# Interleaving the 128-column slices of the stationary operands of a two-layer decoder trunk

## The chip, the cores and the metric

The kernel runs on one core of a Trainium2 chip. The metric is the device time of one execution in microseconds (us); lower is better. The time before the change is 1608.19 us, the median of three runs that lie between 1607.14 and 1608.36 us.

## The reference

A causal decoder trunk of two layers works on x of shape 256 x 2048 in float32. Layer 0 is retention with 8 heads, layer 1 a causal pooling mixer with 4 groups; each ends with an embedding gated by a sigmoid.

```python
def retention_branch(xn, w_in, w_out):
    q, k, v, g = split(xn @ w_in)            # 2048 -> 8 heads x (256 + 256 + 512 + 512)
    ...                                      # rotary q, k; decayed scores; y = scores @ v; group norm
    return (silu(g) * y) @ w_out             # 4096 -> 2048

def pool_branch(xn, w_in, w_group, scale, w_out):
    u, g = split(xn @ w_in)                  # 2048 -> 4096 + 4096
    ...                                      # window means of u minus u -> d
    mixed = einsum('bsgc,gce->bsge', d, w_group) * scale      # 4 groups of 1024 x 1024
    return (mixed * silu(g)) @ w_out         # 4096 -> 2048

def reference(...):
    for i in range(2):
        h = h + branch_i(rms_norm(h, norm_i))
        gate = sigmoid(rms_norm(h, ple_norm[i]) @ ple_w_gate[i])
        h = h + gate * (p[i] @ ple_w_proj[i])
    return rms_norm(h, final_norm)
```

## The kernel before, in words

Every large product has 256 rows (two token tiles t of 128) and streams its weights once from memory. A float32 value is split in two float32r parts, hi and lo, and a product is three matmuls: x_hi by w_hi (L304), x_hi by w_lo (L305) and x_lo by w_hi (L306). The x part is the stationary operand: a slice of 128 columns (the tokens of one tile) by 128 partitions (channels), loaded anew before each matmul. The weight part is the moving operand of 512 columns.

The work is cut in 552 units. A unit holds two channel blocks of 128 by 512 output columns of weights. For each unit ScalarE writes w_hi (L567, a cast of 128x1024), VectorE writes w_lo (L800, a subtraction of 128x1024) and TensorE runs 12 matmuls: two tiles t, two channel blocks b, three products. Four units of w_hi and w_lo are held in a ring (RING = 4). TensorE waits for a unit on `lo_ready`, ScalarE waits before it overwrites a slot on `unit_used`. The unit order is written out by hand in the loops of each engine.

The stationary operands before the change lie in buffers `[P, blocks, SEQ]`, so the 128 columns of a slice are neighbours in the partition's memory:

- `xa_hi`, `xa_lo` (16 blocks x 256): the input of all projections. It is read by 3 passes per head and 4 per group, each of 8 units.
- `oT_hi`, `oT_lo` (8 blocks x 256): the gated branch output, transposed, read by the output projections (8 units per head, 16 per group).
- `xb_hi`, `xb_lo` (16 blocks x 256): the input of the two gate products (32 units each).
- `dT_hi`, `dT_lo`: the window means (8 units per group). `pT_hi`, `pT_lo`: the embedding inputs (4 units per layer).

Who fills them: `h_transposes` transposes a chunk of four blocks of h into two PSUM banks (L327, 8 transposes), `stream_hi` on ScalarE writes the hi part block by block (L587, 4 x 128x256), and `stream_lo` on VectorE writes the lo part, reading PSUM and the hi part (L839, 4 x 128x256). `xT_ready` tells TensorE that a chunk is whole; TensorE waits for it before it reads the chunk, and before the next chunk's transposes. `y_hi_part` and `y_lo_part` (L615, L914, 128x512) fill `oT` for a head, `m_hi_part` and `m_lo_part` (L656, L967, 128x256) for a pooling group.

At the start the order on TensorE is: transposes of chunks 0 and 1, unit 0, transposes of chunk 2, unit 1, transposes of chunk 3, units 2, 3 and on.

Of the kernel before, what the change touches and what calls it, by code (L numbers as in the profile page):

```python
# [92 lines left out]
def trunk(nc, stream, x, pT, gains, pool_scale, final_gain, rope, decay, band, counts, ident, out):  # L93
    with ExitStack() as ctx:
# [22 lines left out]
        w_raw = sb("w_raw", [P, RAW, PIECE * COL], F32)  # L117
        w_hi = sb("w_hi", [P, RING, UNIT * COL], F32R)
        w_lo = sb("w_lo", [P, RING, UNIT * COL], F32R)
        xa_hi = sb("xa_hi", [P, KD, SEQ], F32R)  # L120
        xa_lo = sb("xa_lo", [P, KD, SEQ], F32R)
        oT_hi = sb("oT_hi", [P, KG, SEQ], F32R)
        oT_lo = sb("oT_lo", [P, KG, SEQ], F32R)
        h = sb("h", [P, TT, D], F32)
        emb = sb("emb", [P, TT, D], F32)
        pT_hi = sb("pT_hi", [P, 2, KP, SEQ], F32R)
        pT_lo = sb("pT_lo", [P, 2, KP, SEQ], F32R)
# [30 lines left out]
        dT_hi = at("dT_hi", 8, [P, KG, SEQ], F32R)  # L158
        dT_lo = at("dT_lo", 16, [P, KG, SEQ], F32R)
# [136 lines left out]
        def _(pe):  # L296
            def products(t, s, pair, hi, lo, k0, first, last):

                for b in range(UNIT):
                    xh = hi[:, k0 + b, t * P:(t + 1) * P]  # L300
                    xl = lo[:, k0 + b, t * P:(t + 1) * P]
                    wh = w_hi[:, s, b * COL:(b + 1) * COL]
                    wl = w_lo[:, s, b * COL:(b + 1) * COL]
                    pe.matmul(acc[pair][t][:], xh, wh, start=first and b == 0, stop=False)  # L304
                    pe.matmul(acc[pair][t][:], xh, wl, start=False, stop=False)  # L305
                    mm = pe.matmul(acc[pair][t][:], xl, wh, start=False, stop=last and b == UNIT - 1)  # L306
                return mm
# [179 lines left out]
            def close(layer, base, seg, ou):  # L487

                for c in range(EMB_U):
                    if c >= 2:  # L490
                        pe.wait_ge(e_read, layer * NC + c - 1)
                    if c == 1 and layer == 0:
                        pe.wait_ge(v_ready, HEADS)
                    if c == 0 and layer == 0:
                        pe.wait_ge(p_split, 1)
                    unit(c, base, "AC"[c % 2], pT_hi[:, layer], pT_lo[:, layer], 0, True, True, seg)
# [12 lines left out]
                z0 = layer * NC  # L509
                last = EMB_U + NC * ou + GATE_U  # L510
                if layer == 1:
                    last -= RING
                for u in range(EMB_U, last):
                    c, k = divmod(u - EMB_U, ou)
                    z, kz = divmod(u - EMB_U - NC * ou, KD_U)
                    if c < NC:
                        if k == 0 and c in (1, 2):
                            pe.wait_ge(e_read, z0 + c + 2)
                        if k == 0 and c == 3:
                            pe.wait_ge(h_ready, h0 + 1)  # L520
                        unit(u, base, "BACB"[c], oT_hi, oT_lo, k * UNIT, k == 0, k == ou - 1, seg)
                    else:
                        if kz == 0 and z < 3:
                            pe.wait_ge(h_ready, h0 + z + 2)
                        if kz == 0 and z == 3:
                            pe.wait_ge(z_read, z0 + 2)
                        if z == 0 and kz % 2 == 0:
                            pe.wait_ge(xT_ready, NC * (2 * layer + 1) + kz // 2 + 1)
                        unit(u, base, "ACBC"[z], xb_hi, xb_lo, kz * UNIT, kz == 0, kz == KD_U - 1, seg)
                    for cc in range(NC):  # L530
                        if u == EMB_U + ou * (cc + 1):
                            h_transposes(2 * layer + 1, cc)
                        if cc < NC - 1 and layer == 0 and u == EMB_U + NC * ou + KD_U * (cc + 1) + 1:
                            h_transposes(2, cc)
# [22 lines left out]
        def _(act):  # L557
# [54 lines left out]
            def y_hi_part(hd):  # L612
                act.wait_ge(yT_done, hd + 1)
                for b in range(2):
                    act.copy(oT_hi[:, 2 * b:2 * b + 2, :], side[b][:].rearrange("p (k n) -> p k n", n=SEQ)  # L615
                             ).then_inc(yT_hi, 1)

            def emb_out(layer, c, base):
# [22 lines left out]
            def d_hi_part(n, c):  # L641
                for b in range(2):
                    act.wait_ge(d_scaled, n * 2 + (b + 1))
                    act.copy(dT_hi[:, 4 * c + 2 * b:4 * c + 2 * b + 2, :], d_tmp[:, 2 * b:2 * b + 2, :]).then_inc(d_hi_ready, 1)

            def pg_sigmoid(n, pair, done, first):
                act.wait_ge(unit_used, done)
# [5 lines left out]
            def m_hi_part(n, k0, c):  # L653
                act.wait_ge(mT_done, n + 1)
                for j in range(4):
                    cp = act.activation(oT_hi[:, 4 * c + j, :], side[j // 2][:, (j % 2) * SEQ:(j % 2 + 1) * SEQ], ACT.Copy,  # L656
                                        scale=pscale[:, bass.ds(k0 + j, 1)])
                    if j % 2:
                        cp.then_inc(mT_hi, 1)

            def head(hd, base, first, landings):
                o = 0 if first else NC * RO_U
                for u in range(3 * KD_U + o):
# [129 lines left out]
        def _(dve):  # L793
# [169 lines left out]
            def m_lo_part(n, k0, c):  # L963
                for j in range(4):
                    if j % 2 == 0:
                        dve.wait_ge(mT_hi, n * 2 + (j // 2 + 1))
                    ins = dve.scalar_tensor_tensor(  # L967
                        out=oT_lo[:, 4 * c + j, :], in0=side[j // 2][:, (j % 2) * SEQ:(j % 2 + 1) * SEQ],
                        scalar=pscale[:, bass.ds(k0 + j, 1)], in1=oT_hi[:, 4 * c + j, :].bitcast(F32),
                        op0=ALU.mult, op1=ALU.subtract)  # L970
                ins.then_inc(mT_ready, 1)

            def head(hd, base, first):
                o = 0 if first else NC * RO_U
                for u in range(3 * KD_U + o):
# [279 lines left out]
```

## Time and profile before

| | |
|---|---|
| Median of three runs | 1608.19 us |
| The profiled execution's own time | 1607.45 us |
| Its span, first to last instruction | 1605.6 us |
| TensorE matmul busy | 1584.2 us, 7240 instructions |
| TensorE weight load busy | 1317.9 us, 7240 instructions |
| VectorE busy | 988.2 us |
| ScalarE busy | 727.0 us |
| Mean granted TensorE clock | 0.998 |

Matmul and weight load overlap: they are two rows for one engine. A record's duration includes the time in which an operand travels, and neighbouring records overlap, so the distance between two starts tells more than a duration. The span is 1.9 us shorter than the execution's own time.

### The profile page before, as it was taken

To read this page: it belongs to the slowest core of one execution; us is meant where nothing else is said; L and a number is where in the kernel's file an instruction comes from. 1 tells how busy PE (TensorE), PEld (TensorE's weight loads), DVE (VectorE), ACT (ScalarE), POOL (GpSimd) and SP (SyncE) were. 2 spreads that over 40 slices of the span, in tenths; PEclk is the share of its full clock that TensorE was granted. 3 is DMA by queue.
4 is the path that set the end of the run, shared out by engine and by line. 5 is a ranking of instruction groups with operands and counts; after the bars stand their busy time and mean duration, and the time that the engine had idled before them with its cause. 6 is when DMAs were issued, how large, how long until landed. Compare 5 with 4: busy or idle time off the path is not lost.

```text
span 1605.6 us, 19583 instructions
## 1 busy us (share of the span) xinstructions
PE 1584.2 (99%) x7240; PEld 1317.9 (82%) x7240; DVE 988.2 (62%) x1218; ACT 727.0 (45%) x888; POOL 5.1 (0%) x13
## 2 busy tenths in 40 slices
PE   7999999999999999999999999999999999999997
PEld 6888888888888888888888888888888888888885
DVE  5676666657566666757756555645565555556565
ACT  6444444444443444445655444334434443445553
POOL 0000000000000000000000000000000000000000
PEclk9999999999999999999999999999999999999999
DMA  9444554545455554555455554555555555455551
GB/s 356 172 171 182 184 187 176 187 180 183 183 183 183 183 183 159 207 183 195 166 197 197 186 186 174 198 187 184 183 184 182 200 188 182 179 217 183 184 185 77
DMA packets 42806, 299.24 MB, mean 186 GB/s; under 512 B 4848, under 2 KB 4864, under 8 KB 7312
## 3 DMA queue, kind: packets, MB, share of 16 engines
q1 hardware_dynamic: 41408, 292.60, 50.5%
q0 software_dynamic: 1072, 5.06, 0.8%
q10 hardware_dynamic: 288, 1.05, 0.2%
q8 instruction: 26, 0.43, 0.1%
q14 instruction: 12, 0.10, 0.0%
HBM read 296.60 MB, written 2.10 MB: 186 GB/s over the span
## 4 chain that ended last, share of the span: by engine, by line
PE 98%; DVE 1%; DMA 0%; ACT 0%; issue 0%; SPq 0%; ACTq 0%
PE accB L304 11%; PE accB L305 11%; PE accB L306 11%; PE accA L304 10%; PE accC L304 10%; PE accA L306 10%; PE accA L305 10%; PE accC L305 10%; PE accC L306 10%; PE side L327 2%; DMA h<-in_x_dram 0%; PE side L369 0%; PE side L367 0%; PE side L368 0%; PE side L416 0%; PE side L417 0%
## 5 line engine op out<-in xcount | busy, mean ns | idle before, releaser
L800 DVE TENSOR_TENSOR w_lo<-w_raw,w_hi 128x1024 fp32r<-128x1024 f32 x552 | 669.4, 1222 | 418.7 <-ACT w_hi L567 413.6
L567 ACT CAST w_hi<-w_raw 128x1024 fp32r<-128x1024 f32 x552 | 579.6, 1055 | 620.4 <-PE accB L306 263.7
L304 PE MATMUL accA<-w_hi,xa_hi 128*128 128x512 f32 x512 | 201.4, 393 | 0.9 <-DVE w_lo L800 0.9
L306 PE MATMUL accA<-w_hi,xa_lo 128*128 128x512 f32 x512 | 199.8, 390 | 0.0
L305 PE MATMUL accA<-w_lo,xa_hi 128*128 128x512 f32 x512 | 199.8, 390 | 0.0
L304 PE MATMUL accC<-w_hi,xa_hi 128*128 128x512 f32 x384 | 150.7, 392 | 0.0
L305 PE MATMUL accC<-w_lo,xa_hi 128*128 128x512 f32 x384 | 149.5, 389 | 0.0
L306 PE MATMUL accC<-w_hi,xa_lo 128*128 128x512 f32 x384 | 149.4, 389 | 0.0
L304 PE MATMUL accB<-w_hi,xa_hi 128*128 128x512 f32 x384 | 149.4, 389 | 0.0
L305 PE MATMUL accB<-w_lo,xa_hi 128*128 128x512 f32 x384 | 149.4, 389 | 0.0
L306 PE MATMUL accB<-w_hi,xa_lo 128*128 128x512 f32 x384 | 149.4, 389 | 0.0
L304 PEld LDWEIGHTS accA<-w_hi,xa_hi 128*128 128x128 f32 x512 | 96.6, 189 | 20.9 <-DVE w_lo L800 1.1
L306 PEld LDWEIGHTS accA<-w_hi,xa_lo 128*128 128x128 f32 x512 | 96.4, 188 | 20.2
L305 PEld LDWEIGHTS accA<-w_lo,xa_hi 128*128 128x128 f32 x512 | 96.5, 188 | 19.5
L304 PE MATMUL accB<-w_hi,oT_hi 128*128 128x512 f32 x256 | 99.8, 390 | 0.0
L305 PE MATMUL accB<-w_lo,oT_hi 128*128 128x512 f32 x256 | 99.6, 389 | 0.0
L306 PE MATMUL accB<-w_hi,oT_lo 128*128 128x512 f32 x256 | 99.6, 389 | 0.0
L306 PEld LDWEIGHTS accC<-w_hi,xa_lo 128*128 128x128 f32 x384 | 72.1, 188 | 15.1
L306 PEld LDWEIGHTS accB<-w_hi,xa_lo 128*128 128x128 f32 x384 | 72.1, 188 | 15.0
L304 PEld LDWEIGHTS accB<-w_hi,xa_hi 128*128 128x128 f32 x384 | 72.1, 188 | 15.0
L305 PEld LDWEIGHTS accB<-w_lo,xa_hi 128*128 128x128 f32 x384 | 72.1, 188 | 14.9
L305 PEld LDWEIGHTS accC<-w_lo,xa_hi 128*128 128x128 f32 x384 | 72.1, 188 | 14.4
(183 smaller groups left out, 2114.1 us busy)
## 6 DMA issues: line engine op xcount, KB each, us to landing
w_raw<-in_stream_dram SPq DMA_DIRECT2D x275, 1024.0 KB, 4.7
h<-in_x_dram SPq DMA_DIRECT2D x4, 512.0 KB, 9.1
w_raw<-in_stream_dram SPq DMA_DIRECT2D x2, 512.0 KB, 6.6
dec<-in_decay_dram POOLq DMA_DIRECT2D x1, 1024.0 KB, 8.5
fgain<-in_final_gain_dram POOLq DMA_DIRECT2D x1, 1024.0 KB, 5.0
out_dram<-emb ACTq DMA_DIRECT2D x2, 512.0 KB, 3.0
out_dram<-emb SPq DMA_DIRECT2D x2, 512.0 KB, 2.6
bnd_raw<-in_band_dram POOLq DMA_DIRECT2D x1, 768.0 KB, 7.6
```

Source lines behind the costliest of these rows:

```text
L304: pe.matmul(acc[pair][t][:], xh, wh, start=first and b == 0, stop=False)
L305: pe.matmul(acc[pair][t][:], xh, wl, start=False, stop=False)
L306: mm = pe.matmul(acc[pair][t][:], xl, wh, start=False, stop=last and b == UNIT - 1)
L327: mm = pe.transpose(side[j // 2][:, (j % 2) * SEQ + t * P:(j % 2) * SEQ + (t + 1) * P], src(t)[:, tiles + j * P:tiles + (j + 1) * P], idn[:])
L567: act.copy(w_hi[:, r % RING, :], w_raw[:, r // 2, (r % 2) * 1024:(r % 2 + 1) * 1024]).then_inc(hi_ready, 1)
L800: dve.tensor_tensor(w_lo[:, r % RING, :], w_raw[:, r // 2, (r % 2) * 1024:(r % 2 + 1) * 1024], w_hi[:, r % RING, :].bitcast(F32), ALU.subt ...
```

## The change

Five buffers get their 128-column slices interleaved in groups of `mesh` slices: column i of slice q lies at `buf[:, q // mesh, i, q % mesh]`. A slice is then read, and written, with a step of `mesh` elements of 4 bytes. The steps are 2 for `xa_hi`, 4 for `xa_lo`, 8 for `oT_hi`, 16 for `oT_lo` and 32 for `xb_hi`. The buffers `xb_lo`, `dT_hi`, `dT_lo`, `pT_hi` and `pT_lo` are rewritten with mesh 1, which is the old layout under another shape. Sizes of buffers, their addresses, the number and order of instructions and all waits stay.

```diff
+class Chunks:
+    def __init__(self, buf, mesh):
+        self.buf, self.mesh = buf, mesh
+
+    def one(self, k, t):
+        q = k * TT + t
+        return self.buf[:, q // self.mesh, :, q % self.mesh]
+
+    def some(self, k, n):
+        q = k * TT
+        if self.mesh == 1:
+            return self.buf[:, q:q + n * TT, :, 0]
+        assert q % self.mesh + n * TT <= self.mesh
+        return self.buf[:, q // self.mesh, :, q % self.mesh:q % self.mesh + n * TT].rearrange("p i q -> p q i")
...
-        xa_hi = sb("xa_hi", [P, KD, SEQ], F32R)
-        xa_lo = sb("xa_lo", [P, KD, SEQ], F32R)
-        oT_hi = sb("oT_hi", [P, KG, SEQ], F32R)
-        oT_lo = sb("oT_lo", [P, KG, SEQ], F32R)
+        xa_hi = Chunks(sb("xa_hi", [P, KD * TT // 2, P, 2], F32R), 2)
+        xa_lo = Chunks(sb("xa_lo", [P, KD * TT // 4, P, 4], F32R), 4)
+        oT_hi = Chunks(sb("oT_hi", [P, KG * TT // 8, P, 8], F32R), 8)
+        oT_lo = Chunks(sb("oT_lo", [P, KG * TT // 16, P, 16], F32R), 16)
...
-        xb_hi = at("xb_hi", 0, [P, KD, SEQ], F32R)
-        xb_lo = at("xb_lo", 16, [P, KD, SEQ], F32R)
+        xb_hi = Chunks(at("xb_hi", 0, [P, KD * TT // 32, P, 32], F32R), 32)
+        xb_lo = Chunks(at("xb_lo", 16, [P, KD * TT // 1, P, 1], F32R), 1)
...
-                    xh = hi[:, k0 + b, t * P:(t + 1) * P]
-                    xl = lo[:, k0 + b, t * P:(t + 1) * P]
+                    xh = hi.one(k0 + b, t)
+                    xl = lo.one(k0 + b, t)
...
-                    cp = act.activation(hi[:, k, :], side[j // 2][:, (j % 2) * SEQ:(j % 2 + 1) * SEQ], ACT.Copy,
+                    cp = act.activation(hi.some(k, 1), side[j // 2][:, (j % 2) * SEQ:(j % 2 + 1) * SEQ].rearrange("p (q i) -> p q i", i=P), ACT.Copy,
                                         scale=gain[:, stage, k:k + 1])
...
-                        out=lo[:, k, :], in0=side[j // 2][:, (j % 2) * SEQ:(j % 2 + 1) * SEQ],
-                        scalar=gain[:, stage, k:k + 1], in1=hi[:, k, :].bitcast(F32), op0=ALU.mult, op1=ALU.subtract)
+                        out=lo.some(k, 1), in0=side[j // 2][:, (j % 2) * SEQ:(j % 2 + 1) * SEQ].rearrange("p (q i) -> p q i", i=P),
+                        scalar=gain[:, stage, k:k + 1], in1=hi.some(k, 1).bitcast(F32), op0=ALU.mult, op1=ALU.subtract)
```

The other writers (L615, L656, L914, L967, and those of `dT` and `pT`) are changed in the same way: `some` in place of the slice, and the PSUM or source operand seen as slices of 128.

## Rows read from the trace of the kernel before

**Rows 1.** The page: busy time by engine, and the chain that ended last.

```profile
PE 1584.2 (99%) x7240; PEld 1317.9 (82%) x7240; DVE 988.2 (62%) x1218; ACT 727.0 (45%) x888; POOL 5.1 (0%) x13
...
PEclk9999999999999999999999999999999999999999
...
PE 98%; DVE 1%; DMA 0%; ACT 0%; issue 0%; SPq 0%; ACTq 0%
```

**Rows 2.** Waits of TensorE: line and releaser, us in total, times, longest.

```profile
PE side L327 <- DMA idn<-in_ident_dram: 5.2, 1, 5.2
PE side L327 <- DMA h<-in_x_dram: 3.4, 1, 3.4
PE accA L304 <- DVE w_lo L800: 0.9, 2, 0.7
```

**Rows 3.** Timeline, 299.7 to 303.8 us, 19 matmuls and their loads: start, us, instruction.

```profile
299.73 0.39 PE L305 MATMUL accB<-w_lo,oT_hi 128*128 128x512 f32 x1
...
302.23 0.19 PEld L305 LDWEIGHTS accC<-w_lo,oT_hi 128*128 128x128 f32 x1
...
302.45 0.39 PE L305 MATMUL accC<-w_lo,oT_hi 128*128 128x512 f32 x1
...
303.81 0.39 PE L305 MATMUL accC<-w_lo,oT_hi 128*128 128x512 f32 x1
```

**Rows 4.** Timeline inside the scores of head 0, where matmuls are short.

```profile
57.05 0.28 PE L358 MATMUL side<-qkT_lo,qkT_hi 128*128 128x256 f32 x1
57.17 0.28 PE L359 MATMUL side<-qkT_hi,qkT_lo 128*128 128x256 f32 x1
...
57.77 0.19 PEld L359 LDWEIGHTS side<-qkT_hi,qkT_lo 128*128 128x128 f32 x1
...
58.21 0.19 PEld L304 LDWEIGHTS accC<-w_hi,xa_hi 128*128 128x128 f32 x1
```

**Rows 5.** Groups of weight loads by line and operands: count, busy us, mean ns, idle.

```profile
L304 PEld LDWEIGHTS accA<-w_hi,xa_hi 128*128 128x128 f32 x512 | 96.6, 189 | 20.9 <-DVE w_lo L800 1.1 <-issue 0.4
...
L304 PEld LDWEIGHTS accB<-w_hi,oT_hi 128*128 128x128 f32 x256 | 48.0, 188 | 10.2 <-issue 0.3
...
L304 PEld LDWEIGHTS accC<-w_hi,xb_hi 128*128 128x128 f32 x128 | 24.0, 188 | 4.9
```

**Rows 6.** Groups of VectorE and ScalarE instructions: count, busy us, mean ns, idle.

```profile
L839 DVE SCALAR_TENSOR_TENSOR xa_lo<-side,gain,xa_hi 128x256 fp32r<-128x256 f32 x32 | 13.2, 476 | 13.4 <-ACT xa_hi L587 13.4
...
L878 DVE SCALAR_TENSOR_TENSOR v_lo<-accC,rs,v_hi 128x512 fp32r<-128x512 f32 x16 | 11.3, 746 | 9.0 <-ACT v_hi L595 9.0
...
L587 ACT ACTIVATE xa_hi<-side,gain 128x256 fp32r<-128x256 f32 x32 | 12.5, 471 | 8.2 <-PE side L327 8.2
```

**Rows 7.** Timeline of VectorE, 0 to 26 us: `stream_lo` of the four chunks.

```profile
8.22 1.66 DVE L839 SCALAR_TENSOR_TENSOR xa_lo<-side,gain,xa_hi 128x256 fp32r<-128x256 f32 x4 [8.22 <-ACT xa_hi L587]
...
13.39 1.66 DVE L839 SCALAR_TENSOR_TENSOR xa_lo<-side,gain,xa_hi 128x256 fp32r<-128x256 f32 x4 [2.37 <-ACT xa_hi L587]
...
18.23 1.66 DVE L839 SCALAR_TENSOR_TENSOR xa_lo<-side,gain,xa_hi 128x256 fp32r<-128x256 f32 x4 [1.94 <-ACT xa_hi L587]
```

**Rows 8.** Timeline of TensorE, 0 to 26 us: transposes of chunks 1 to 3, unit 3.

```profile
10.52 1.97 PE L327 MATMUL side<-idn,h 128*128 128x128 f32 x8 [3.35 <-DMA h<-in_x_dram]
...
16.28 1.04 PE L327 MATMUL side<-idn,h 128*128 128x128 f32 x8
...
20.04 1.06 PE L327 MATMUL side<-idn,h 128*128 128x128 f32 x8
...
24.96 0.50 PE L304 MATMUL accA<-w_hi,xa_hi 128*128 128x512 f32 x1 [0.69 <-DVE w_lo L800]
```

**Rows 9.** Timeline of VectorE, 744 to 800 us: the first `xb` chunk of layer 0.

```profile
755.27 1.66 DVE L839 SCALAR_TENSOR_TENSOR xb_lo<-side,gain,xb_hi 128x256 fp32r<-128x256 f32 x4 [2.05 <-ACT xb_hi L587]
```

**Rows 10.** Timeline of TensorE, 756 to 782 us: the transposes of the next `xb` chunk.

```profile
759.66 1.03 PE L327 MATMUL side<-idn,h 128*128 128x128 f32 x8
```

More of the change, by code:

```diff
@@ L119, in trunk @@
         w_lo = sb("w_lo", [P, RING, UNIT * COL], F32R)
-        xa_hi = sb("xa_hi", [P, KD, SEQ], F32R)
-        xa_lo = sb("xa_lo", [P, KD, SEQ], F32R)
-        oT_hi = sb("oT_hi", [P, KG, SEQ], F32R)
-        oT_lo = sb("oT_lo", [P, KG, SEQ], F32R)
+        xa_hi = Chunks(sb("xa_hi", [P, KD * TT // 2, P, 2], F32R), 2)
+        xa_lo = Chunks(sb("xa_lo", [P, KD * TT // 4, P, 4], F32R), 4)
+        oT_hi = Chunks(sb("oT_hi", [P, KG * TT // 8, P, 8], F32R), 8)
+        oT_lo = Chunks(sb("oT_lo", [P, KG * TT // 16, P, 16], F32R), 16)
         h = sb("h", [P, TT, D], F32)
         emb = sb("emb", [P, TT, D], F32)
-        pT_hi = sb("pT_hi", [P, 2, KP, SEQ], F32R)
-        pT_lo = sb("pT_lo", [P, 2, KP, SEQ], F32R)
+        pT_hi = sb("pT_hi", [P, 2, KP * TT, P, 1], F32R)
+        pT_lo = sb("pT_lo", [P, 2, KP * TT, P, 1], F32R)
         sig = sb("sig", [P, TT, COL], F32)
@@ L151, in trunk @@
         pr_lo = at("pr_lo", 44, [P, SEQ + P], F32R)
-        xb_hi = at("xb_hi", 0, [P, KD, SEQ], F32R)
-        xb_lo = at("xb_lo", 16, [P, KD, SEQ], F32R)
+        xb_hi = Chunks(at("xb_hi", 0, [P, KD * TT // 32, P, 32], F32R), 32)
+        xb_lo = Chunks(at("xb_lo", 16, [P, KD * TT // 1, P, 1], F32R), 1)
         u_hi = at("u_hi", 0, [P, TT, COL], F32R)
         u_lo = at("u_lo", 4, [P, TT, COL], F32R)
-        dT_hi = at("dT_hi", 8, [P, KG, SEQ], F32R)
-        dT_lo = at("dT_lo", 16, [P, KG, SEQ], F32R)
+        dT_hi = Chunks(at("dT_hi", 8, [P, KG * TT // 1, P, 1], F32R), 1)
+        dT_lo = Chunks(at("dT_lo", 16, [P, KG * TT // 1, P, 1], F32R), 1)
         gm = at("gm", 24, [P, 2, TT, COL], F32)
@@ L495, in close @@
                         pe.wait_ge(p_split, 1)
-                    unit(c, base, "AC"[c % 2], pT_hi[:, layer], pT_lo[:, layer], 0, True, True, seg)
+                    unit(c, base, "AC"[c % 2], Chunks(pT_hi[:, layer], 1), Chunks(pT_lo[:, layer], 1), 0, True, True, seg)
                     if c == 2 and layer == 0:
@@ L614, in y_hi_part @@
                 for b in range(2):
-                    act.copy(oT_hi[:, 2 * b:2 * b + 2, :], side[b][:].rearrange("p (k n) -> p k n", n=SEQ)
+                    act.copy(oT_hi.some(2 * b, 2), side[b][:].rearrange("p (q i) -> p q i", i=P)
                              ).then_inc(yT_hi, 1)
@@ L643, in d_hi_part @@
                     act.wait_ge(d_scaled, n * 2 + (b + 1))
-                    act.copy(dT_hi[:, 4 * c + 2 * b:4 * c + 2 * b + 2, :], d_tmp[:, 2 * b:2 * b + 2, :]).then_inc(d_hi_ready, 1)
+                    act.copy(dT_hi.some(4 * c + 2 * b, 2), d_tmp[:, 2 * b:2 * b + 2, :].rearrange("p k (t i) -> p (k t) i", i=P)).then_inc(d_hi_ready, 1)
             def pg_sigmoid(n, pair, done, first):
@@ L655, in m_hi_part @@
                 for j in range(4):
-                    cp = act.activation(oT_hi[:, 4 * c + j, :], side[j // 2][:, (j % 2) * SEQ:(j % 2 + 1) * SEQ], ACT.Copy,
+                    cp = act.activation(oT_hi.some(4 * c + j, 1), side[j // 2][:, (j % 2) * SEQ:(j % 2 + 1) * SEQ].rearrange("p (q i) -> p q i", i=P), ACT.Copy,
                                         scale=pscale[:, bass.ds(k0 + j, 1)])
@@ L670, in head @@
                         act.wait_ge(p_landed, 16)
-                        act.copy(pT_hi[:], p_raw).then_inc(p_hi, 1)
+                        act.copy(pT_hi[:].rearrange("p l q i one -> p (l q i one)"), sig[:].rearrange("p t n -> p (t n)")).then_inc(p_hi, 1)
                     if not first and u == 2:
@@ L913, in y_lo_part @@
                     dve.wait_ge(yT_hi, hd * 2 + (b + 1))
-                    ins = dve.tensor_tensor(oT_lo[:, 2 * b:2 * b + 2, :], side[b][:].rearrange("p (k n) -> p k n", n=SEQ),
-                                            oT_hi[:, 2 * b:2 * b + 2, :].bitcast(F32), ALU.subtract)
+                    ins = dve.tensor_tensor(oT_lo.some(2 * b, 2), side[b][:].rearrange("p (q i) -> p q i", i=P),
+                                            oT_hi.some(2 * b, 2).bitcast(F32), ALU.subtract)
                 ins.then_inc(yT_ready, 1)
@@ L943, in d_lo_part @@
                     dve.wait_ge(d_hi_ready, n * 2 + (b + 1))
-                    ks = slice(4 * c + 2 * b, 4 * c + 2 * b + 2)
-                    ins = dve.tensor_tensor(dT_lo[:, ks, :], d_tmp[:, 2 * b:2 * b + 2, :], dT_hi[:, ks, :].bitcast(F32),
-                                            ALU.subtract)
+                    k = 4 * c + 2 * b
+                    ins = dve.tensor_tensor(dT_lo.some(k, 2), d_tmp[:, 2 * b:2 * b + 2, :].rearrange("p k (t i) -> p (k t) i", i=P),
+                                            dT_hi.some(k, 2).bitcast(F32), ALU.subtract)
                 ins.then_inc(d_ready, 1)
@@ L967, in m_lo_part @@
                     ins = dve.scalar_tensor_tensor(
-                        out=oT_lo[:, 4 * c + j, :], in0=side[j // 2][:, (j % 2) * SEQ:(j % 2 + 1) * SEQ],
-                        scalar=pscale[:, bass.ds(k0 + j, 1)], in1=oT_hi[:, 4 * c + j, :].bitcast(F32),
+                        out=oT_lo.some(4 * c + j, 1), in0=side[j // 2][:, (j % 2) * SEQ:(j % 2 + 1) * SEQ].rearrange("p (q i) -> p q i", i=P),
+                        scalar=pscale[:, bass.ds(k0 + j, 1)], in1=oT_hi.some(4 * c + j, 1).bitcast(F32),
                         op0=ALU.mult, op1=ALU.subtract)
@@ L982, in head @@
                         dve.wait_ge(p_hi, 1)
-                        dve.tensor_tensor(pT_lo[:], p_raw, pT_hi[:].bitcast(F32), ALU.subtract).then_inc(p_split, 1)
+                        dve.tensor_tensor(pT_lo[:].rearrange("p l q i one -> p (l q i one)"), sig[:].rearrange("p t n -> p (t n)"),
+                                          pT_hi[:].rearrange("p l q i one -> p (l q i one)").bitcast(F32), ALU.subtract).then_inc(p_split, 1)
                     if not first and u == 2:
```

## The prediction

> **What bounds the kernel.** I read the page first. Matmuls are busy for 1584.2 of 1605.6 us, the granted clock is full in all slices but for rounding (level 2.4 GHz), and the chain that ended last is TensorE for 98% [rows 1]. The waits of TensorE then say how often another engine stops it: 8.6 us for the first transfers and 0.9 us for a late w_lo, all in the first 25 us [rows 2]. So the time is the number of matmuls times the distance between two of them, plus a start. The timeline gives that distance: 19 matmuls of 512 columns start between 299.73 and 303.81 us, 4.08 / 18 = 227 ns apart [rows 3]. 512 columns at 2.4 GHz are 213 ns; some 13 ns are a gap, which the 256-column matmuls show too: 120 ns against 107 [rows 4].
>
> A weight load runs beside the matmul before its own: the load of L305 starts at 302.23 and its matmul at 302.45 [rows 3]. Its 188 ns [rows 5] are a time with travel in it. How long the load path is taken is seen where matmuls are short: five loads start from 57.77 to 58.21 us, 0.44 / 4 = 110 ns apart, and there they set the pace [rows 4]. So a load of neighbouring columns takes 110 of the 227 ns, and 117 ns are free. A load costs nothing until it takes 227 / 110 = 2.06 times as long as now; beyond that, each 0.1 of the factor k costs 11 ns per load. The whole case hangs on where k lies for a stepped read.
>
> **The change part by part.** No instruction, byte or wait is added, and the weights, the moving operand and the DMAs are untouched. Three things change.
>
> *The stepped loads.* xa is read by 3 x 8 + 4 x 4 = 40 passes of 8 units, 4 pairs (t, b) each: 1280 loads per line (the accA row with 512 is 16 of the 40 passes [rows 5]). L304 and L305 both load the hi part. That makes 2560 loads with step 2 (xa_hi) and 1280 with step 4 (xa_lo). oT has 8 x 8 + 4 x 16 = 128 units: 1024 loads with step 8 and 512 with step 16. xb has 64 units: 512 loads with step 32. In all 5888 loads are stepped, 3328 of them by 4 or more elements and 2048 by 8 or more. No row shows a stepped load. The nearest is the plain one, k = 1, and it gives no upper end; a reader that must spend two turns where it spent one would give k = 2, three turns k = 3. The cost is 5888 or 3328 times (110 k - 227) ns where that is positive, else nothing. At k = 2 the load takes 220 ns, 7 ns less than the distance of the matmuls: free, barely. I take k at or below 2, cost 0, since the slot holds all of a doubling. The ends are 0 and, at k = 3, 3328 x 103 ns = 343 us.
>
> The Trainium skill ("SBUF — State Buffer", section "Door 1: The DMA port swizzle") says that SBUF lines have 16 bytes, that two hits on a line are needed for full rate and that an access that goes to a new line pays. By it xa_hi, two elements of 4 bytes to a line, stays free, and the 3328 loads with a step of 4 or more pay an amount that the section does not give. No row here bears on it, and its sum would be mine as long as the penalty stays under a doubling.
>
> *The stepped writes and reads of ScalarE and VectorE.* An L839 of 256 columns takes 476 ns and an instruction of the same kind with 512 takes 746 [rows 6], so 256 columns are 270 ns of it, about 1.05 ns each. If a stepped operand halves its rate, d = 270 ns are added to an L839, and a = 270 ns to an L587 if its step of 2 counts as well. Below, both are 0. For most of the run that is covered: 64 L839, 32 L967 and 16 L914 of twice the size add at most 34 us to VectorE, which is idle for 617 us [rows 1], and as much to ScalarE, and the ring holds units in advance. The tightest place in the middle is layer 0 with xb: VectorE ends a chunk at 755.27 + 1.66 = 756.93 and TensorE starts the next transposes, which wait for it, at 759.66 [rows 9, 10]. 2.7 us are free and 2 a + 4 d = 1.6 are needed.
>
> At the start it is not covered. Chunks 0, 1 and 2 are done on VectorE at 9.88, 15.05 and 19.89 us [rows 7], and TensorE begins the transposes that wait for them at 10.52, 16.28 and 20.04 [rows 8]: 0.6, 1.2 and 0.15 us free. Chunk 3 has nothing free, since unit 3 waits for the w_lo behind it on VectorE and starts late, at 24.96 [rows 8]. Each chunk adds 2 a + 4 d (VectorE starts after two of ScalarE's four). Together that is 4 (2 a + 4 d) - 2.0 us. I take d = 270 ns for step 4 in xa_lo and a = 0 for step 2: 4.3 - 2.0 = 2.3 us. The ends are 0, and 6.5 - 2.0 = 4.5 us. TensorE never waits afterwards, so nothing is made up.
>
> *The buffers with mesh 1.* Same addresses, same order, 0 us.
>
> **The sum.** Span 1605.6 + 0 + 2.3 = 1607.9, with 1.9 us around it 1609.8. The profiled execution was 0.7 us under the median of the runs, so about 1610 us. The runs differ by 1.2 us, and 0.2% (3.2 us) is about what a measurement of this kernel can tell from no change.
>
> **The rivals.**
> 1. *The load just misses its slot.* The 13 ns gap that sits between matmuls may sit between long loads too: 220 + 13 = 233 ns, 6 ns over, for 3328 loads 20 us, 1630 us with the start. It decides from k = 2.06, or from a gap over 7 ns at k = 2. For it: the slot is full to 7 ns. Against: at 110 ns the loads come 3 ns from 128 columns at 1.2 GHz (107 ns), with no such gap. Range 1613 to 1640.
> 2. *k between 2.1 and 2.6, or k = 3 for steps of 8 and more only.* The first gives up to 3328 x 59 ns = 197 us, 1807 us; the second 2048 x 103 = 211 us, 1821 us. If step 2 pays too, k = 2.4 for all 5888 loads is 5888 x 37 = 218 us, 1828 us. For it: a stepped element has no neighbour to be fetched with. Against: no row.
> 3. *k = 3 for all steps of 4 or more:* 1610 + 343 = 1953 us. TensorE would go at 330 ns on every second or third matmul.
> 4. *Step 2 pays as well,* k = 3 for all 5888 loads: 606 us, 2216 us. For it speaks only that its elements are no neighbours either.
> 5. *Faster.* If the 13 ns gap comes from the load and the moving read meeting in one memory, another order of addresses might take it away: at most 5888 x 13 ns = 77 us, 1531 us. Against: the gap is the same for 256 and 512 columns.
> 6. *The change does nothing,* because the compiler undoes the layout: excluded, since the step stands in each operand's access pattern.
>
> The skill's page "Vector Engine (DVE) Microarchitecture Reference", section 5.2, has for VectorE that single elements with hops between them cost 1.7 to 2.5 ns in place of 1.05, and only adjacent pairs are free. By that rule all 5888 loads pay, as in the last case of rival 2; as an estimate, its factors of 1.6 to 2.4 would give from nothing to that case's 218 us. No run here shows it for TensorE.
>
> **How the numbers follow.** The load stays in its slot: 0.48, of which 0.39 with the start under 3.2 us and 0.09 above. Rival 1: 0.20. Rival 2: 0.13. Rival 3: 0.09. Rival 4: 0.04. Faster: 0.06. That makes same 0.39, slower 0.55, faster 0.06. The predicted time is that of the likeliest case, 1610 us, whose own range is 1607 to 1613 us. The range 1605 to 1830 leaves out rivals 3, 4 and 5 (0.19).
>
> **What the profile after would show.** Right: loads of oT and xb that record a longer time than 188 ns, matmul starts still 227 ns apart in the same stretch, L839 at some 750 ns, and unit 3 starting 2 us later than 24.96. Wrong: matmul starts further apart, and then by buffer: accB with oT against accB with xa in the timeline tells steps of 8 and 16 from 2 and 4, and L304 against L306 tells hi from lo. What would upset it most is a k above 2.06 for any step, since thousands of loads multiply it; least, a mistake on ScalarE or VectorE.

## The result and the profile after

The changed kernel takes 1665.9 us (median of four runs, 1665.62 to 1666.71) against 1607.95 us for the kernel before (the median of four runs now, one more than above): 58 us more, ratio 1.036 with an interval of 1.0348 to 1.0372. The time lies inside the predicted range (1605 to 1830), but well outside that of the likeliest case (1607 to 1613). It is closest in kind to rival 1 (a load that just misses its slot), with almost three times its price.

Line numbers are 18 higher now: L304 to L306 are L322 to L324, L327 is L345, L839 is L857, L800 is L818. From the page, busy times by engine and the chain [rows 1]:

```profile
PE 1639.2 (98%) x7240; PEld 1505.2 (90%) x7240; DVE 1012.5 (61%) x1218; ACT 741.8 (45%) x888; POOL 5.1 (0%) x13
...
PE 96%; DVE 2%; DMA 1%; ACT 0%; issue 0%; SPq 0%; ACTq 0%
```

The same number of instructions, TensorE still the bound, and weight loads busy for 187 us more. So the question is again the distance of two matmuls, from start to start. The timeline of TensorE after the change, first and last of three stretches (start, us, instruction) [rows 3]:

```profile
299.74 0.39 PE L324 MATMUL accA<-w_hi,xa_lo 128*128 128x512 f32 x1
...
305.28 0.40 PE L324 MATMUL accA<-w_hi,xa_lo 128*128 128x512 f32 x1
305.52 0.41 PE L322 MATMUL accB<-w_hi,oT_hi 128*128 128x512 f32 x1
...
315.91 0.41 PE L323 MATMUL accC<-w_lo,oT_hi 128*128 128x512 f32 x1
```

```profile
837.96 0.39 PE L322 MATMUL accC<-w_hi,xb_hi 128*128 128x512 f32 x1
...
845.95 0.39 PE L323 MATMUL accC<-w_lo,xb_hi 128*128 128x512 f32 x1
```

Between the first two rows lie 24 distances, 231 ns each; between the next two 43, 242 ns each; in the last stretch 34, 235 ns each. In the same passages before it was 227. Taken over all matmuls of 512 columns after 30 us, leaving out distances over 330 ns, the means before and after are 227.4 and 232.8 ns with xa, 227.3 and 241.6 with oT, 227.3 and 234.8 with xb, and 227.7 and 228.1 with dT, whose layout did not change. So 3840 x 5.4 = 20.7 us, 1536 x 14.3 = 22 us and 768 x 7.5 = 5.8 us: 48 to 49 of the 58 us are matmuls that follow each other more slowly.

The groups of weight loads after the change (count, busy us, mean ns, idle) [rows 5]:

```profile
L324 PEld LDWEIGHTS accA<-w_hi,xa_lo 128*128 128x128 f32 x512 | 157.8, 308 | 19.4
L322 PEld LDWEIGHTS accA<-w_hi,xa_hi 128*128 128x128 f32 x512 | 100.7, 197 | 2.1 <-DVE w_lo L818 1.5 <-issue 0.2
L323 PEld LDWEIGHTS accB<-w_lo,oT_hi 128*128 128x128 f32 x256 | 84.3, 329 | 0.0
...
L324 PEld LDWEIGHTS accB<-w_hi,oT_lo 128*128 128x128 f32 x256 | 80.1, 313 | 0.0
...
L322 PEld LDWEIGHTS accC<-w_hi,xb_hi 128*128 128x128 f32 x128 | 39.1, 305 | 5.7
```

Loads with a step of 4 or more record 117 to 141 ns more than the 188 before; step 2 records 5 to 8 ns more. A plain load takes the load path for 110 ns, so the longer ones look like a doubling and some more. The longest is step 8, not step 32.

The waits of TensorE (us in total, times, longest) [rows 2]:

```profile
PE accB L322 <- issue: 2.0, 2, 1.2
PE accA L322 <- DVE w_lo L818: 1.2, 1, 1.2
PE side L345 <- DVE h L1096: 0.8, 3, 0.3
...
PE side L345 <- DVE xa_lo L857: 0.5, 1, 0.5
```

Three of the four are new. The writers (VectorE, then ScalarE) show why [rows 6]:

```profile
L985 DVE SCALAR_TENSOR_TENSOR oT_lo<-side,pscale,oT_hi 128x256 fp32r<-128x256 f32 x32 | 21.2, 727 | 21.2 <-ACT oT_hi L674 21.2
...
L932 DVE TENSOR_TENSOR oT_lo<-side,oT_hi 128x512 fp32r<-128x512 f32 x16 | 18.5, 1205 | 19.6 <-ACT oT_hi L633 19.6
...
L857 DVE SCALAR_TENSOR_TENSOR xa_lo<-side,gain,xa_hi 128x256 fp32r<-128x256 f32 x32 | 17.6, 680 | 14.4 <-ACT xa_hi L605 14.4
```

```profile
L633 ACT CAST oT_hi<-side 128x512 fp32r<-128x512 f32 x16 | 17.3, 1202 | 20.0 <-PE side L345 20.0
L605 ACT ACTIVATE xa_hi<-side,gain 128x256 fp32r<-128x256 f32 x32 | 12.7, 486 | 10.3 <-PE side L345 10.3
```

Before, these took 476 ns (L985, then L967), 686 (L932, then L914), 476 (L857, then L839), 590 (L633, then L615) and 471 (L605, then L587). A step of 4 or more costs VectorE 0.8 ns more per column where only what it writes or only what it reads is stepped so widely (672 ns for xa_lo in only_xa_lo, 681 for xb_lo), and 1.0 where both are (L985, L932); it costs ScalarE's writes 1.0 to 1.2 ns. ScalarE's step 2 costs 15 ns per instruction, nearly nothing, and a VectorE that reads xa_hi at step 2 takes 477 ns in only_xa_hi (experiment 2), as before. At the start unit 3 begins 2.5 us later than the 24.96 of [rows 8], of which 0.9 us are a later first transfer (the second transposes start at 11.44 in place of 10.52):

```profile
27.43 0.51 PE L322 MATMUL accA<-w_hi,xa_hi 128*128 128x512 f32 x1 [1.19 <-DVE w_lo L818]
```

### The profile page after: what moved, and what is told of

The parts are those of the page before. It is cut to its first block, busy times and chain, and to the rows that moved or that the text cites. A ratio compares the mean times of both kernels' runs of the same rounds, so it can differ in the third digit from the quotient of the medians.

```text
span 1664.9 us, 19583 instructions
## 1 busy us (share of the span) xinstructions
PE 1639.2 (98%) x7240; PEld 1505.2 (90%) x7240; DVE 1012.5 (61%) x1218; ACT 741.8 (45%) x888; POOL 5.1 (0%) x13
## 3 DMA queue, kind: packets, MB, share of 16 engines
q10 hardware_dynamic: 288, 1.05, 0.2%
## 4 chain that ended last, share of the span: by engine, by line
PE 96%; DVE 2%; DMA 1%; ACT 0%; issue 0%; SPq 0%; ACTq 0%
PE accB L323 11%; PE accB L322 11%; PE accB L324 11%; PE accC L322 10%; PE accA L323 10%; PE accA L322 10%; PE accC L323 10%; PE accC L324 10%; PE accA L324 10%; PE side L345 2%; DMA h<-in_x_dram 1%; DVE xb_lo L857 0%; DVE w_lo L818 0%; PE side L385 0%; PE side L386 0%
## 5 line engine op out<-in xcount | busy, mean ns | idle before, releaser
L818 DVE TENSOR_TENSOR w_lo<-w_raw,w_hi 128x1024 fp32r<-128x1024 f32 x552 | 668.7, 1223 | 426.0 <-ACT w_hi L585 422.3
L322 PE MATMUL accA<-w_hi,xa_hi 128*128 128x512 f32 x512 | 203.8, 398 | 1.2 <-DVE w_lo L818 1.2
L323 PE MATMUL accA<-w_lo,xa_hi 128*128 128x512 f32 x512 | 203.7, 398 | 0.0
L324 PE MATMUL accA<-w_hi,xa_lo 128*128 128x512 f32 x512 | 202.1, 395 | 0.0
L324 PEld LDWEIGHTS accA<-w_hi,xa_lo 128*128 128x128 f32 x512 | 157.8, 308 | 19.4
L323 PE MATMUL accB<-w_lo,xa_hi 128*128 128x512 f32 x384 | 152.8, 398 | 0.0
L322 PE MATMUL accC<-w_hi,xa_hi 128*128 128x512 f32 x384 | 152.1, 396 | 0.0
L323 PE MATMUL accC<-w_lo,xa_hi 128*128 128x512 f32 x384 | 152.1, 396 | 0.0
L322 PE MATMUL accB<-w_hi,xa_hi 128*128 128x512 f32 x384 | 151.3, 394 | 0.0
L324 PE MATMUL accC<-w_hi,xa_lo 128*128 128x512 f32 x384 | 151.1, 393 | 0.0
L324 PE MATMUL accB<-w_hi,xa_lo 128*128 128x512 f32 x384 | 150.6, 392 | 0.0
L324 PEld LDWEIGHTS accB<-w_hi,xa_lo 128*128 128x128 f32 x384 | 118.3, 308 | 15.4
L324 PEld LDWEIGHTS accC<-w_hi,xa_lo 128*128 128x128 f32 x384 | 118.3, 308 | 14.2
L323 PEld LDWEIGHTS accA<-w_lo,xa_hi 128*128 128x128 f32 x512 | 99.9, 195 | 17.6
L322 PE MATMUL accB<-w_hi,oT_hi 128*128 128x512 f32 x256 | 104.9, 410 | 2.0 <-issue 2.0
L323 PE MATMUL accB<-w_lo,oT_hi 128*128 128x512 f32 x256 | 104.4, 408 | 0.0
L322 PEld LDWEIGHTS accA<-w_hi,xa_hi 128*128 128x128 f32 x512 | 100.7, 197 | 2.1 <-DVE w_lo L818 1.5
L324 PE MATMUL accB<-w_hi,oT_lo 128*128 128x512 f32 x256 | 102.1, 399 | 0.0
L323 PEld LDWEIGHTS accC<-w_lo,xa_hi 128*128 128x128 f32 x384 | 74.6, 194 | 13.0
L323 PEld LDWEIGHTS accB<-w_lo,xa_hi 128*128 128x128 f32 x384 | 74.1, 193 | 13.4
L323 PEld LDWEIGHTS accB<-w_lo,oT_hi 128*128 128x128 f32 x256 | 84.3, 329 | 0.0
```

Source lines behind the costliest of these rows:

```text
L818: dve.tensor_tensor(w_lo[:, r % RING, :], w_raw[:, r // 2, (r % 2) * 1024:(r % 2 + 1) * 1024], w_hi[:, r % RING, :].bitcast(F32), ALU.subt ...
```

## The experiments

The matmul kernels below leave out the whole trunk: they only run matmuls on part of one weight matrix. The edits of the full kernel start from the changed one, and each puts every buffer that it does not name back to mesh 1.

**1. The length of a stepped load, and who disturbs whom.** Theory A says that the load path decides, theory B that other engines' traffic does. The loop is that of mix_idle and mix_busy; steps_alone has 1 in place of 3.

```diff
+            for s, (n, steps) in enumerate(SETS):
+                for r in range(REP):
+                    for b in range(3):
+                        step = steps[(3 * r + b) % len(steps)]
+                        mm = pe.matmul(ps[s % 8][:, 0:n], load(step, r), mov[:, (b % 2) * 512:(b % 2) * 512 + n],
+                                       start=True, stop=True)
```

> This kernel holds only matmuls: 64 of 128 moving columns and 64 of 512 for each step 1, 2, 3, 4, 8, 16, 32 and 64 of the stationary slice, with every other engine idle. At 128 columns the load sets the pace, so the distance of two starts is the load's occupancy. Both theories: 110 ns for steps 1 and 2, about 220 ns for steps of 4 and more (the loads recorded 308 ns against 188, 120 more). Theory A, the load path decides (a doubled load plus the gap of some 13 ns overruns its slot): at 512 columns about 233 to 242 ns for steps of 4 and more, 227 for 1 and 2, although all other engines are idle. Theory B, the load fits its slot and is slowed only by what ScalarE, VectorE or the DMAs do in the same memory: 227 ns at 512 columns for all steps. Step 3 tells whether it is the number of elements in 16 bytes or only the neighbour that counts.

> Only matmuls of 512 columns, other engines idle, 72 for each pattern of steps: 1; 2; 4; 8; then the kernel's own mixes (1,1,4), (2,2,4), (8,8,16) and (32,32,1). Theory A: 227 ns for 1 and 2, 233 to 242 for 4 and 8, and in the mixes only the matmul behind a long load is late, so (2,2,4) averages some 230 to 233 and (8,8,16) some 242, as in the changed kernel. Theory B: 227 ns in all.

> The same matmuls, with ScalarE casting 128x1024 and VectorE subtracting 128x1024 in turn all the while, as in the kernel (no DMA). Theory A: the same distances as with idle engines. Theory B: 230 to 242 ns for patterns with steps of 4 and more, 227 for steps 1 and 2.

From steps_alone, the timeline of TensorE: one row is 64 matmuls of 512 columns with steps 2, 3, 4, 8, 16, 32 and 64 (banks c to h, then a). The distance is the difference of two starts over 64.

```profile
171.48 15.10 PE L60 MATMUL bankc<-mov,stat 128*128 128x512 f32 x64
186.42 15.23 PE L60 MATMUL bankd<-mov,stat 128*128 128x512 f32 x64
201.49 15.21 PE L60 MATMUL banke<-mov,stat 128*128 128x512 f32 x64
216.53 15.85 PE L60 MATMUL bankf<-mov,stat 128*128 128x512 f32 x64
232.21 15.30 PE L60 MATMUL bankg<-mov,stat 128*128 128x512 f32 x64
247.35 15.30 PE L60 MATMUL bankh<-mov,stat 128*128 128x512 f32 x64
262.49 15.24 PE L60 MATMUL banka<-mov,stat 128*128 128x512 f32 x64
```

Step 2 gives 14.94 / 64 = 233 ns, step 3 235, step 4 235, step 8 245, step 16 237, step 32 237. The stretches of 128 columns went at 213 ns for steps 1, 2 and 3, about twice the 110 ns of [rows 4], and at 233, 240 and 221 ns for steps 4, 8 and 16. The granted clock reads 1.00, but the next matmuls, of 512 columns, start 427 ns apart, which is 1.2 GHz, so the lower level is likely for the short ones before them too. The short loads were measured again, in experiment 3.

The timeline of mix_idle, 72 matmuls per row with steps 1, 2 and 4, then that of mix_busy with steps 1 and 2.

```profile
46.59 16.48 PE L60 MATMUL bankb<-mov,stat 128*128 128x512 f32 x72
62.91 16.96 PE L60 MATMUL bankc<-mov,stat 128*128 128x512 f32 x72
79.72 17.09 PE L60 MATMUL bankd<-mov,stat 128*128 128x512 f32 x72
```

```profile
45.33 16.48 PE L60 MATMUL bankb<-mov,stat 128*128 128x512 f32 x72
61.66 16.96 PE L60 MATMUL bankc<-mov,stat 128*128 128x512 f32 x72
```

Both have 227 ns for step 1 and 233 for step 2, and the durations agree in all eight patterns (mix_busy has ScalarE and VectorE at work beside, but no DMA traffic). Theory B falls: with every other engine idle the slow distances are all there. The mixes give 232 ns for (1,1,4), 231 for (2,2,4), 241 for (8,8,16) and 235 for (32,32,1), close to the kernel's 233 for xa, 242 and 235. But A as it stood falls too: it had 227 ns for step 2.

**2. One buffer at a time.** In each, the other buffers go back to mesh 1:

```diff
-        xa_lo = Chunks(sb("xa_lo", [P, KD * TT // 4, P, 4], F32R), 4)
+        xa_lo = Chunks(sb("xa_lo", [P, KD * TT, P, 1], F32R), 1)
```

> The changed layout for xa_hi alone (step 2, 2560 loads). Theory A (16 bytes hold two elements, so step 2 is free): 1608 to 1610 us, matmuls 227 ns apart in all passes. Rival (step 2 pays too, part of the 5.6 ns per xa matmul is its own): 3840 x 1 to 4 ns, 1612 to 1623 us.

> Step 4 for xa_lo alone (1280 loads). Theory A: 1280 x 17 ns = 21 us plus 2 us at the start, 1629 to 1632 us. Rival (step 2 shares the cost): 1612 to 1622 us.

> Steps 8 and 16 for oT_hi and oT_lo alone (1536 loads). Theory A: 1536 x 14.3 ns = 22 us, start as before, 1630 us. Rival that the slow writes of oT on ScalarE and VectorE delay TensorE: more than 1632, with waits of TensorE on them in the list.

> Step 32 for xb_hi alone (512 loads). The loads cost 768 x 7.5 = 6 us. In layer 0 the four chunks have TensorE waiting for the residual sums queued on VectorE behind the stepped instructions (7.2 us between transposes against 6.3): about 2 us more. 1615 to 1617 us; without that wait 1613 to 1614.

| Stepped | us | more than before (1608.02) | ratio, interval |
|---|---|---|---|
| xa_hi, step 2 | 1630.1 | 22 | 1.014 (1.0123 to 1.0157) |
| xa_lo, step 4 | 1630.4 | 22 | 1.0142 (1.0125 to 1.0159) |
| oT, steps 8, 16 | 1634.4 | 26 | 1.0167 (1.015 to 1.0184) |
| xb_hi, step 32 | 1617.4 | 9 | 1.0058 (1.0041 to 1.0074) |

Step 2 alone costs 22 us: A and the 16-byte reading of it missed that one. On xa_lo A hit the time, but not the way: its 17 ns were the extra of all xa matmuls put down to the 1280 with a stepped load, and the trace of only_xa_lo has the extra on all three matmuls of a product, 6.7 ns on L324 (the stepped load), 2.8 on L322 and 6.8 on L323, whose loads are plain. The mean distance with xa is 233.4 ns in only_xa_hi and 232.8 in only_xa_lo, 232.8 with both in the changed kernel, so the two do not add. The time of only_oT is that of its rival, more than 1632 us with waits on the slow writes. Its loads are 1536 x 14.4 = 22 us (241.7 ns against 227.3) and 4 us are left; its timeline shows one of the places:

```profile
754.10 2.19 DVE L932 TENSOR_TENSOR oT_lo<-side,oT_hi 128x512 fp32r<-128x512 f32 x2 [1.51 <-ACT oT_hi L633]
...
756.39 0.60 PE L322 MATMUL accB<-w_hi,oT_hi 128*128 128x512 f32 x1 [0.79 <-issue]
```

VectorE is done with oT_lo at 754.10 + 2.19 = 756.29, and TensorE starts 0.1 us later after 0.79 us of idling (the profile names no releaser, but the code waits there for `yT_ready`). That is the last head's output at the end of layer 0, where only the four embedding units cover the chain. The last group's output at the end of layer 1 has the same with 1.20 us of idling; the two cost 2.2 us. Another 1.5 us are 11 places at which the second matmul of 512 columns behind a run of short ones comes 413 to 448 ns after the first, against 283 or 314 before in nearly all; the runs do not say why. In only_xb_hi, a little over its 1615 to 1617 us, 5.8 of the 9 us are distances; the list of waits has 2.0 us for the residual sums of h (L1096), which VectorE takes in its order behind the stepped L857.

**3. Where the load's length ends and something else begins.** short_bursts has this loop; half_loads varies the width of the slice; oT_16 is only_oT with the mesh of `oT_hi` set to 16.

```diff
+                for q in range(4):
+                    for r in range(24):
+                        pe.matmul(ps[0][:], load(1, r), mov[:, (r % 2) * 512:(r % 2) * 512 + 512], start=True, stop=True)
+                    for r in range(12):
+                        mm = pe.matmul(ps[1 + s % 7][:, 0:n], load(step, r), mov[:, (r % 2) * 512:(r % 2) * 512 + n],
+                                       start=True, stop=True)
```

> Bursts of 12 short matmuls (128, then 256 moving columns) behind 24 plain ones of 512 that keep TensorE's pace, four bursts per step 1, 2, 4, 8, 16, 32, 64. At 128 columns the load sets the distance: 110 ns for step 1. If a load of step 4 has two turns per column, 215 to 235; step 8, which is the slowest with 512 columns (245 ns), 240 or more, so that its loads and not its matmuls pace it; step 2 110 ns if step 2 is free on the load path, some 140 and more if neighbours are what counts.

> Only matmuls, other engines idle, 48 per setting. First 512 moving columns with stationary slices of 128, 64 and 32 columns at steps 1, 2, 4, 8, 16, 32; then 256 moving columns with 128. A smaller slice has a shorter load. Theory A (the load path decides): with 64 or 32 columns every load fits its slot and all steps go back to 227 ns. Theory C (each stepped read of the load disturbs the read of the moving columns): the extra over step 1 shrinks in proportion, from 7 ns at step 2 and 8 at step 4 to 3 to 4 ns at 64 and 2 at 32 columns. Theory D (a stepped load costs a fixed time at its start): the extra stays 7 to 8 ns at every size. With 256 moving columns (slot 118 ns) steps 1 and 2 should give 118 and 125, steps of 4 and more the load itself, 220 to 240.

> As only_oT, but oT_hi with step 16 in place of 8 (oT_lo 16 as before). Theory A with a load of its own length for each step: the matmul kernels gave 236.6 ns for step 16 and 245 for step 8, so 1024 x 8 ns = 7 to 8 us less than only_oT, 1627 us. Rival (what counts is only that the step is 4 or more): the same 1634 us.

The weight loads of short_bursts: a row of 12 loads for short matmuls (128 columns; steps 1, 2 and 4 on banks b to d), and the row of plain loads behind it.

```profile
42.50 1.53 PEld L61 LDWEIGHTS bankb<-mov,stat 128*128 128x128 f32 x12
43.95 1.01 PEld L59 LDWEIGHTS banka<-mov,stat 128*128 128x128 f32 x5
...
69.90 1.60 PEld L61 LDWEIGHTS bankc<-mov,stat 128*128 128x128 f32 x12
71.43 0.76 PEld L59 LDWEIGHTS banka<-mov,stat 128*128 128x128 f32 x4
...
98.69 2.89 PEld L61 LDWEIGHTS bankd<-mov,stat 128*128 128x128 f32 x12
101.48 0.56 PEld L59 LDWEIGHTS banka<-mov,stat 128*128 128x128 f32 x3
```

The load is what sets the pace here, so the distance of two load starts is its length. At steps 1 and 2 the second load still waits for a long matmul, 227 and 229 ns after the first; the other eleven distances are (1.45 - 0.23) / 11 = 111 ns for step 1 and 118 for step 2. Step 4 has 2.79 / 12 = 233 ns; in the same way step 8 has 238 and step 16 221. The timeline of half_loads has longer stretches, 48 matmuls of 256 columns with steps 4, 8, 16 and 32:

```profile
252.87 11.37 PE L58 MATMUL bankf<-mov,stat 128*128 128x256 f32 x48
264.07 11.72 PE L58 MATMUL bankg<-mov,stat 128*128 128x256 f32 x48
275.63 10.87 PE L58 MATMUL bankh<-mov,stat 128*128 128x256 f32 x48
286.34 10.94 PE L58 MATMUL banka<-mov,stat 128*128 128x256 f32 x48
```

They give 233, 241, 223 and 225 ns; steps 1 and 2 go at 120 there, the pace of the 256-column matmuls themselves. So against the kernel's slot of 227 ns the load of step 8 overruns by 14 ns and that of step 4 by 6 ns; those of step 16 and 32 fit by 2 to 4 ns only, and that of step 2 is not even near. At step 16 a load of 223 ns and a gap of 13 would make the 237 ns seen, which is rival 1's mechanism; but at steps 4 and 8 the same sum would make 246 and 254 ns, and 235 and 245 were measured.

half_loads rules out C and D in turn: with slices of 64 columns and 512 moving ones, where no load can overrun, plain slices go at 230 ns, step 2 at 227, steps 4 to 32 at 232 to 233; with 32 columns, plain ones at 232 and step 8 at 227. The extra is neither proportional nor fixed, and the plain loads have it as well. Step 8 falls from 245 ns with 128 columns to 232 with 64, so its overrun is real; step 4 falls only from 235 to 233.

oT_16 gave 1626.4 us (ratio 1.0115, 1.0098 to 1.0132), 8.0 us less than only_oT, with a mean distance of 236.7 ns with oT: as predicted, the step-8 part, 1024 x 8 ns, can be taken away by itself.

**4. The 227 ns as the exception.** This gave theory E: 227 ns is what a load of 128 neighbouring columns gets, and any other load leaves it.

```diff
+            for s, (m, step, first, turn, swap) in enumerate(SETS):
+                for r in range(REP):
+                    j = first + (r % step if turn else 0)
+                    k = (r % 2) * 512 if swap else 0
+                    mm = pe.matmul(ps[s % 8][0:m, :], stat[:, j:j + m * step:step] if step > 1 else stat[:, j:j + m],
+                                   mov[:, k:k + 512], start=True, stop=True)
```

> 36 matmuls of 512 columns per setting, other engines idle: plain slices of 128, 96, 64, 48, 32 and 112 columns, plain slices from other starts, step 2 with the start fixed and turning, step 16, step 4 with 112 columns, and some with the moving operand fixed. Theory E (227 ns is the exception, held only by a load of 128 neighbouring columns; any other length or timing of the load gives 230 to 234): plain 96, 64, 48, 32 and 112 columns give 230 to 234, whatever the bank, and so does step 2. Theory C (each extra visit of the load to the memory costs): plain slices of any length give 227 or less, step 2 more. If the start or the moving operand decides, the settings with another start or with the moving operand fixed differ from their neighbours in the list. Step 4 with 112 columns has a load of about 204 ns that fits its slot: 230 to 234 by E, against 235 with 128.

> Step 2 for xa_hi and step 4 for xa_lo, the rest plain. If the extras of the two added up: 22 + 22 = 44 us, 1652 us. If, as theory E has it, one stepped load in three already takes the whole passage out of its 227 ns and further ones add little: 1631 to 1634 us, the two or three above only_xa_lo being the start.

The timeline of load_length, rows of 36 matmuls of 512 columns. First plain slices of 128, 96, 64, 48 and 32 columns; then plain 128 columns that begin 1, 2 and 64 elements further on; then 128 columns with step 2, twice; last 112 columns with step 4 and plain:

```profile
37.74 8.32 PE L64 MATMUL bankb<-mov,stat 128*128 128x512 f32 x36
45.91 8.45 PE L64 MATMUL bankc<-mov,stat 128*96 128x512 f32 x36
54.19 8.44 PE L64 MATMUL bankd<-mov,stat 128*64 128x512 f32 x36
62.47 8.64 PE L64 MATMUL banke<-mov,stat 128*48 128x512 f32 x36
70.94 8.49 PE L64 MATMUL bankf<-mov,stat 128*32 128x512 f32 x36
...
95.72 8.53 PE L64 MATMUL banka<-mov,stat 128*128 128x512 f32 x36
104.08 8.47 PE L64 MATMUL bankb<-mov,stat 128*128 128x512 f32 x36
112.39 8.33 PE L64 MATMUL bankc<-mov,stat 128*128 128x512 f32 x36
...
137.00 8.64 PE L64 MATMUL bankf<-mov,stat 128*128 128x512 f32 x36
145.49 8.64 PE L64 MATMUL bankg<-mov,stat 128*128 128x512 f32 x36
...
212.76 8.62 PE L64 MATMUL bankg<-mov,stat 128*112 128x512 f32 x36
221.22 8.42 PE L64 MATMUL bankh<-mov,stat 128*112 128x512 f32 x36
```

128 columns take 8.17 / 36 = 227 ns. The shorter plain slices are slower: 230 for 96 and for 64, 235 for 48. The same 128 columns from one element on take 232, from two elements on 231, and from 64 elements on 227 again. Step 2 takes 236 (8.49 / 36), whether the start turns or the moving operand stays. Fixing the moving operand or changing the bank changes nothing, and 64 columns at step 2 give 227. So E holds as a description, that 227 ns is the exception, and not as a rule: 128 neighbouring columns from one or two elements on lose it, and 64 columns at step 2 and, in half_loads, 32 at step 8 have it. C falls for good: a load with less to read is not faster. Step 4 with 112 columns takes 235 ns, as with 128. Its load is 233 x 112 / 128 = 204 ns by estimate (it records 280 ns against 310 for 128 columns in half_loads) and fits the slot, so at step 4 the overrun is not what makes the 235 ns. One caution: the same loop at step 2 gave 233.3 ns in half_loads and 235.6 here, so 2 ns between two kernels are not a difference of the layout.

xa_both gave 1632.7 us (ratio 1.0155, 1.0138 to 1.0172), inside E's 1631 to 1634, where adding would have given 1652. Once some of the loads of a passage are stepped, the whole passage has left 227 ns. Its 2.6 us over only_xa_hi are the start: unit 3 begins at 27.12 us against 24.70. Not all of that is the change, since the first transfers differ from run to run: in the four kernels with a plain xa (the one before, only_oT, only_xb_hi, oT_16) unit 3 begins between 24.96 and 26.98 us. Counted from the second transposes it begins 14.4 us later in the kernel before, 16.0 in the changed one and 16.1 in xa_both.

## Why the prediction was right in its range and wrong in its centre

- **The range held, partly by its width.** 1666 us lies between what rival 1 prices (to 1640) and the upper prices of rival 2 (1807 to 1828). Rival 2 gives it for k = 2.2 at all 3328 loads, which those of steps 16 and 32 (2.0) do not have. With the measured lengths the prediction's own rule gives 1280 x 6 + 1024 x 14 ns = 22 us.
- **The bound** was right: the time is a count of matmuls times their distance, and the step changes the distance. 48 to 49 of 58 us are that. (The kernel before also waits 0.8 us for qk, L857, later than the first 25 us, which the prediction passed over; after the change that wait is 0.5.)
- **The occupancy of a plain load** (110 ns) was right: 111.
- **"I take k at or below 2, cost 0"** is the term that failed first. By the long stretches k is 2.12 at step 4 (233 / 110), 2.19 at step 8 and 2.03 at step 16. The threshold of 2.06 lies among them. The doubling was right; the remainder of 3 to 21 ns, which I had left out, makes the loads of steps 4 and 8 longer than the slot. Only at step 8 do the runs show a cost of that, 8 ns for each of 1024 loads, 8 us in all; at step 4 a load that fits is as slow.
- **"A load costs nothing until it takes 2.06 times as long"** failed too, and that is the bigger part. A load of step 2 is busy for 118 of the 227 ns and costs 22 us; steps 16 and 32 fit their slot, if barely, and cost 7 to 10 ns per matmul. The step read 227 ns as 213 of matmul and a constant gap of 13. The gap is not constant: it is 13 ns for one way of loading and 17 to 23 for most others. [Rows 3, 4] could not show it, since every matmul of 512 columns in that trace had a load of the one kind. Rival 5 had the thought that the gap depends on how the load is read, with the wrong sign.
- **Rival 1** priced 3328 loads at 6 ns, 20 us. A load that just misses its slot is shown for step 8 only, and the gap of 13 ns behind a long load for none for certain (experiment 3); the 2560 loads of step 2 and all matmuls between stepped loads pay too.
- **The rule of 16-byte lines** in the Trainium skill ("SBUF — State Buffer", section "Door 1: The DMA port swizzle"), two hits for full rate, is borne out for the load path but for 7 ns: step 2 takes 118 ns against 111, step 4 takes 233. Step 3 belongs to neither in its text; its matmul distance was 235 ns, and its load lies between: in steps_alone, with 512 moving columns, it records 253 ns against 193 at step 2 and 309 at step 4. What the rule says nothing of is that the matmul behind an almost full-rate stepped load comes later. The reading of that rule as "xa_hi stays free" was wrong by 22 us.
- **Rivals 2 to 4.** Rival 2's lower end did occur in the loads: k is 2.12 and 2.19 at steps 4 and 8. A k of 2.4 or 3 did not. The factors of 1.6 to 2.4 that were worked out from the Trainium skill ("Vector Engine (DVE) Microarchitecture Reference", section 5.2) fit the loads of step 4 and more (2.0 to 2.2) and not those of step 2 (1.06), which by that rule pay as well. VectorE itself agrees with the page where it steps by 4 or more: 1.05 ns per column and 0.8 to 1.0 more.
- **Stepped writes:** 270 ns for an L839 was taken, 204 measured (680 against 476); 540 for 512 columns, 519 measured; ScalarE's step 2 free, 15 ns measured.
- **The start:** 2.3 us predicted, 2.5 measured, but 0.9 of these are the later first transfer. The other 1.6 fit the prediction's rule with the measured instructions, 4 x (2 x 0.015 + 4 x 0.204) - 2.0 = 1.4 us; that the sum came out near 2.3 was luck.
- **"For most of the run that is covered"** was wrong in two places, worth 2.2 us for oT and, in only_xb_hi, 2.0 us for xb. I had looked at the wait for xT_ready (2.7 us free) and not at what stands behind the stepped instructions on VectorE: the residual sum L1096, for which TensorE's next transposes wait, and the oT chain of the last head and the last group, which only four units cover.

The parts measured alone add up to 25.0 (xa_both) + 26.4 + 9.4 = 61 us, against 58. The traces before and after have the same 7240 matmuls in the same order, and their spans differ by 59.3 us. Start by start, 2.5 us of that come before unit 3; 2.2 at the two waits for oT; 1.3 at the three transposes of xb that wait for L1096 (0.8 in the list of waits, against 2.0 in only_xb_hi); 2.1 at 16 places where the second matmul of 512 columns behind short ones is late; and 51 in all other distances.

**Open:** why 128 neighbouring columns from element 0 or 64, 64 columns at step 2 and 32 at step 8 keep 227 ns, and no other setting tried does. The runs exclude other engines, the PSUM bank, the moving operand's address and the amount read. They leave the timing of the load's reads against the matmul's own, which no run varied by itself: that is a guess, not shown.

## What to carry to other kernels

Keep the stationary operand as neighbouring columns from an aligned start: in a stream of float32r matmuls of 512 columns, stepping it costs 6 to 18 ns of 227 per matmul even where the load seems to have half of its slot free. That one engine has free time beside another does not show that using it costs nothing: look for a row in which its work differs and the other's pace stays the same before pricing a change at nothing. And when instructions on a side engine get longer, walk its queue: who waits for the instruction behind them is the cost.

## What the runs showed of the hardware that was not expected

- The dependence on the step is not monotonic: with 512 moving columns 227 (1), 233 to 236 (2), 235 (3, 4), 245 (8), 237 (16, 32).
- A plain stationary slice of 64 or 96 columns makes matmuls of 512 columns slower (230 ns) than one of 128 (227 ns), and a start one element off costs 5 ns (232).
- The longer loads did not follow TensorE's clock. In steps_alone, where matmuls of 512 columns behind the short ones still start 427 ns apart (1.2 GHz), plain loads take 213 ns and those of steps 4, 8 and 16 take 233, 240 and 221; in short_bursts, behind matmuls 227 ns apart (2.4 GHz), it is 111 against 233, 238 and 221. The granted clock reads 1.00 in both stretches.
- A second matmul of 512 columns behind a run of short ones came 414 to 444 ns after the first with a load of step 8 or 32, against 283 or 314 in the same places before.
